# Forming the last output tile's sum in the matrix engine's banks, with its copies and stores on three engines

## The reference

```
x = x + rmsnorm(f, prm['ln_ffn_post'][i])
x = x + jax.nn.sigmoid(x @ prm['w_ple_gate'][i]) * (pe[i] @ prm['w_ple'][i])
```

## Time and profile before

| | us |
|---|---|
| median of 3 runs | 1069.44 (1069.35 to 1069.86) |
| the profiled execution's own time | 1069.43 |
| its span, first to last instruction | 1067.6 |
| PE busy in the span | 1057.3 |
| DVE busy | 671.6 |
| ACT busy | 550.6 |
| POOL busy | 216.2 |

### The profile page before, as it was taken

How to read it: one execution, slowest core, us unless ns; L and a number is a source line. 1 busy time by engine, 2 the same in 40 slices (tenths; PEclk the granted TensorE clock), 3 DMA queues, 4 the chain that set the end, 5 groups by cost and what they waited for, 6 DMA issues and landing times.

```text
span 1067.6 us, 20384 instructions
## 1 busy us (share of the span) xinstructions
PE 1057.3 (99%) x7347; PEld 1041.7 (98%) x7347; DVE 671.6 (63%) x1236; ACT 550.6 (52%) x940; POOL 216.2 (20%) x348
## 2 busy tenths in 40 slices
PE   8999999999999999999999999999999999999998
PEld 8889999999999999999999999999999999999998
DVE  6876557777777753333977665657777777433365
ACT  6565475555555543335666545655555555433353
POOL 7300022222322320002200102212223322110000
PEclk9999999999999999999999999999999999999999
DMA  9623253555555555545454344366555554545532
GB/s 258 171 72 88 89 158 102 163 157 161 153 151 145 153 148 153 149 148 159 120 158 127 102 125 135 94 136 170 160 156 144 151 157 142 152 145 156 156 101 70
DMA packets 281926, 150.39 MB, mean 141 GB/s; under 512 B 5592, under 2 KB 278816, under 8 KB 281872
## 3 DMA queue, kind: packets, MB, share of 16 engines
q1 hardware_dynamic: 279184, 144.20, 48.0%
q0 software_dynamic: 2544, 5.40, 1.7%
q10 hardware_dynamic: 144, 0.05, 0.0%
HBM read 145.54 MB, written 4.08 MB: 140 GB/s over the span
## 4 chain that ended last, share of the span: by engine, by line
PE 94%; DVE 2%; ACT 2%; DMA 1%; issue 1%; SPq 0%; DVEq 0%; ACTq 0%
PE bank L658 27%; PE bank L660 27%; PE bank L659 27%; PE bank L685 3%; PE bank L688 1%; PE bank L698 1%; PE bank L1029 1%; DMA raw<-in_w_att_in 1%; ACT wh L1177 1%; DVE wl L1504 1%; PE bank L931 1%; PE bank L1070 0%; PE bank L714 0%; PE bank L1072 0%; PE bank L1071 0%
## 5 line engine op out<-in xcount | busy, mean ns | idle before, releaser
L1504 DVE TENSOR_TENSOR wl<-raw,wh 128x1024 fp32r<-128x1024 f32 x270 | 332.4, 1231 | 253.3 <-ACT wh L1177 251.0
L658 PE MATMUL bank<-hH,wh 128*128 128x320 f32 x1280 | 399.5, 312 | 0.2
L660 PE MATMUL bank<-hH,wl 128*128 128x320 f32 x1280 | 395.5, 309 | 0.0
L659 PE MATMUL bank<-hL,wh 128*128 128x320 f32 x1280 | 395.4, 309 | 0.0
L1177 ACT ACTIVATE wh<-raw 128x1024 fp32r<-128x1024 f32 x270 | 284.6, 1055 | 167.5 <-PE bank L660 158.1
L658 PEld LDWEIGHTS bank<-hH,wh 128*128 128x128 f32 x1280 | 240.3, 188 | 1.3 <-issue 0.4
L659 PEld LDWEIGHTS bank<-hL,wh 128*128 128x128 f32 x1280 | 240.4, 188 | 0.2
L660 PEld LDWEIGHTS bank<-hH,wl 128*128 128x128 f32 x1280 | 240.2, 188 | 0.0
L658 PE MATMUL bank<-hidden_hi,wh 128*128 128x320 f32 x720 | 223.5, 310 | 0.5 <-ACT mix L1381 0.5
L660 PE MATMUL bank<-hidden_hi,wl 128*128 128x320 f32 x720 | 222.5, 309 | 0.0
L659 PE MATMUL bank<-hidden_lo,wh 128*128 128x320 f32 x720 | 222.5, 309 | 0.0
(11 more groups left out here) (371 smaller groups left out, 1028.4 us busy)
## 6 DMA issues: line engine op xcount, KB each, us to landing
raw<-in_w_ffn_up SPq DMA_DIRECT2D x128, 512.0 KB, 4.1
raw<-in_w_ffn_down SPq DMA_DIRECT2D x64, 512.0 KB, 4.0
raw<-in_w_rec_in SPq DMA_DIRECT2D x24, 512.0 KB, 3.9
raw<-in_w_att_in SPq DMA_DIRECT2D x18, 512.0 KB, 5.0
raw<-in_w_ple_gate SPq DMA_DIRECT2D x16, 512.0 KB, 4.0
raw<-in_w_att_out SPq DMA_DIRECT2D x8, 512.0 KB, 3.8
raw<-in_w_rec_out SPq DMA_DIRECT2D x8, 512.0 KB, 4.0
raw<-in_w_ple SPq DMA_DIRECT2D x4, 512.0 KB, 3.6
```

Source lines behind the costliest of these rows:

```text
L658: mmul(out, a, rh[:, k, :], start=first, stop=False)
L659: mmul(out, a, rl[:, k, :], start=False, stop=False)
L660: m = mmul(out, b, rh[:, k, :], start=False, stop=last)
L1504: V.tensor_tensor(wl[:, u % R, :], raw[:, u % R, :], wh[:, u % R, :].bitcast(F32), ALU.subtract).then_inc(lo_ready, 1)
```

## The change

The last tile's sum is no longer formed by DVE in `xT`. PE now multiplies the residual `xT[:, 7, ...]` by the identity into a bank and leaves the group open, then multiplies the gated product `sgb[:, 1, ...]` by the identity into the same places with accumulation, so that the bank holds the turned sum. The addition of line 1979 falls away for that one tile. The tile is split into two groups with banks of their own: `("y_end", 0)`, the prompt part, in bank 4, and `("y_end", 1)`, the sample part, in bank 5. DVE copies the prompt part and SP stores it; ACT copies the sample part, waits for its own copy and stores it from its own queue. The sample store of `turn_y(1)`, which SP issued, goes to POOL.

The diff is cut to its core; its pieces stand in the order PE, ACT, DVE, SP, POOL.

```
-            gi = gid("y_end")
-            bank_free(pe, gi)
-            pe.wait_ge(sem("x_out1"), 8)
-            for t, (t0, n) in enumerate(TOK):
-                m = trans(gbank(gi)[0:n, t * P:(t + 1) * P], xT[:, 7, t0:t0 + n], ident[:])
-            m.then_inc(done(gi), 1)
+            parts = (gid("y_end", 0), TOK[:2]), (gid("y_end", 1), TOK[2:])
+            for gi, tokens in parts:
+                bank_free(pe, gi)
+                for t, (t0, n) in enumerate(tokens):
+                    mmul(gbank(gi)[0:n, t * P:(t + 1) * P], xT[:, 7, t0:t0 + n], ident[:], start=t == 0, stop=False,
+                         skip_group_check=True)
+            pe.wait_ge(sem("sg"), 16)
+            for gi, tokens in parts:
+                for t, (t0, n) in enumerate(tokens):
+                    m = mmul(gbank(gi)[0:n, t * P:(t + 1) * P], sgb[:, 1, t0:t0 + n], ident[:], start=False, stop=True,
+                             skip_group_check=True)
+                m.then_inc(done(gi), 1)
...
+                        if i == 7:
+                            gi = gid("y_end", 1)
+                            bank_full(act, gi)
+                            A(xtok[0:TS, 2, 896:D], gbank(gi)[0:TS, 0:P], ACT.Copy).then_inc(sem("y_end_sample"), 1)
+                            act.wait_ge(sem("y_end_sample"), 1)
+                            act.dma_start(O["y_sample"][0, :, 896:D], xtok[0:TS, 2, 896:D]).then_inc(sem("y_stored"), 16)
...
-                    V.tensor_tensor(xT[:, i, :], xT[:, i, :], sgb[:, i % 2, :], ALU.add).then_inc(sem(f"x_out{l}"), 1)
+                    if l == 0 or i < 7:
+                        V.tensor_tensor(xT[:, i, :], xT[:, i, :], sgb[:, i % 2, :], ALU.add).then_inc(sem(f"x_out{l}"), 1)
...
-                for t in range(3):
+                for t in range(3 - half):
...
-            sp.wait_ge(sem("y_end"), 2)
-            sp.dma_start(O["y_sample"][0, :, 896:D], xtok[0:TS, 2, 896:D]).then_inc(sem("y_stored"), 16)
...
+            pool.wait_ge(sem("ytok"), 6)
+            pool.dma_start(O["y_sample"][0, :, y_columns(1)], xtok[0:TS, 2, y_columns(1)]).then_inc(sem("y5_stored"), 16)
+            pool.wait_ge(sem("y5_stored"), 16)
```

More of the change, by code:

```diff
@@ L126, in group_order @@
         o += [(f"gate{l}", i) for i in range(8 if l == 0 else 7)]
-    return o + [("y", 0), ("y", 1), ("y", 2), ("gate1", 7), ("y", 3), ("y", 4), ("y", 5), ("y_end", 0)]
+    return o + [("y", 0), ("y", 1), ("y", 2), ("gate1", 7), ("y", 3), ("y", 4), ("y", 5), ("y_end", 0), ("y_end", 1)]
 GROUPS = {key: n for n, key in enumerate(group_order())}
@@ L137, in group_banks @@
     fixed.update({("o", s): 7 for s in range(8)})
+    fixed.update({("y_end", 0): 4, ("y_end", 1): 5})
     fixed.update({(f"ple{l}", i): 4 + i for l in range(2) for i in (2, 3)})
@@ L462, in _ @@
                     sp.dma_start(dst[:, c], xtok[0:TOK[t][1], t, c]).then_inc(sem("y_stored"), 16)
-            sp.wait_ge(sem("y_end"), 1)
+            sp.wait_ge(sem("y_end_prompt"), 1)
             sp.dma_start(O["y_prompt"][0, :, 896:D].rearrange("(t p) c -> p t c", p=P), xtok[:, 0:2, 896:D]).then_inc(sem("y_stored"), 16)
-            sp.wait_ge(sem("y_end"), 2)
-            sp.dma_start(O["y_sample"][0, :, 896:D], xtok[0:TS, 2, 896:D]).then_inc(sem("y_stored"), 16)
-            sp.wait_ge(sem("y_stored"), 16 * 8)
+            sp.wait_ge(sem("y_stored"), 16 * 7)
         @block.gpsimd
@@ L1984, in _ @@
                     lo(UNITS[f"gate{l}"] + i + R)
-            gi = gid("y_end")
+            gi = gid("y_end", 0)
             bank_full(dve, gi)
-            V.tensor_copy(xtok[:, 0:2, 896:D], gbank(gi)[:, 0:2 * P].rearrange("p (t c) -> p t c", t=2)).then_inc(sem("y_end"), 1)
-            V.tensor_copy(xtok[0:TS, 2, 896:D], gbank(gi)[0:TS, 2 * P:3 * P]).then_inc(sem("y_end"), 1)
+            V.tensor_copy(xtok[:, 0:2, 896:D], gbank(gi)[:, 0:2 * P].rearrange("p (t c) -> p t c", t=2)).then_inc(sem("y_end_prompt"), 1)
 _OUTS = [
```

## The result

The changed kernel takes 1073.18 us (median of 7 runs, 1073.09 to 1073.22), the kernel before 1069.44 in the same session (7 runs, 1069.26 to 1070.07). The ratio is 1.0034, with a 95% interval of 1.0024 to 1.0043: slower by 3.74 us, or 0.34%. The forecast was 1068.7 and the top of its range 1069.8. The span of the profiled execution grew from 1067.6 to 1071.3, so all of the loss lies inside the span.

The account below looks back on a forecast made before the run. PE bounds the kernel, so only the 4.27 us tail behind its last gate matmul can change; last landing 1066.5 plus 0.36 gives span 1066.86, 0.74 less, time about 1068.7, range 1068.1 to 1069.8.

Parts of the forecast that it names:

- the sentence on POOL's store: Moved sample store of tiles 4 to 6: starts at 1064.23, lands at 1066.33, its wait holding up only the program's end.
- SP's 0.36: Program's end: 0.36 us from the last landing to the span's end, taken from the kernel before.
- The 0.17 for the shared transfer engines: Last stores: sharing 16 transfer engines puts the last landing at 1066.5, where the queues alone gave 1066.33.
- The cover holds but for 0.02 us: PE behind the gate: three residual matmuls fit before the product arrives, costing only 0.02 us.
- the 0.113: PE's last tile: step in us of one plain matmul, taken to be the same as a transpose's.
- POOL's store becomes the last: Rival, program's end: a POOL flight of 3.4 to 4.2 lands last, time 1069.8 to 1070.6; range 1069.0 to 1070.6, chance 0.17.
- its deciding point of 3.0: POOL's moved store: a flight of 3.0 us or more costs the whole gain.
- The plain matmuls are slow: Rival, PE's last tile: plain matmuls at four times the transposes' pace, step 0.45 us, time 1070.3; chance 0.06.
- ACT's store is the late one: Rival, last sample store: an ACT flight of 2.95 us from 1064.29 leaves the time at 1069.4; chance 0.07.
- The addition's place: Chain behind the gate: without DVE's sum, 0.54 us goes and PE could start on the product 0.14 after its end.
- POOL's flight of 2.1: Moved store of tiles 4 to 6: 2.1 us from issue to landing, as SP's 96 KB store took.
- Slower by over 0.2%: Whole kernel: needs a POOL flight of over 5.1 us or several rivals together; chance 0.04.

Follow-up runs that it names:

- The kernel with separate transposes: Changed kernel with residual and product each turned by transposes, DVE adding the product, sample store of tiles 4 to 6 on SP: 1069.85 against 1069.54 us, ratio 1.0001.

## Why the prediction was wrong

**The sum was made up to the wrong end.** The step that failed is the sentence on POOL's store: "Nothing else stands behind its wait in POOL's stream, so that holds up only the program's end." The program's end is just what was being predicted, and a DRAIN of 4.3 us stands behind that wait. The sum went from the last landing to the end by SP's 0.36, which is the price of SP's closing. POOL's closing has another, and its row, 5.0 us at 1013.0 with 0.8 of an operation in it, was in the trace of before. It wasn't read, since in a kernel whose POOL ends 50 us early it decides nothing. By it the sum would have been: POOL's landing as forecast, 1066.33, plus 0.15 and 0.3 (as in the profile after) and 4.2 to 5.0 between them, a span of 1071.0 to 1071.8 and a time of 1072.8 to 1073.6; 1073.18 was measured. The 0.17 for the shared transfer engines played no part in the answer: of the three last stores POOL's landed first, and the end hung on it.

**The residual matmuls don't hide.** "The cover holds but for 0.02 us" failed by its size: they hold PE for some 0.6 beyond the product's arrival. The pace in the earlier trace rows was read per row count, six in 0.83, and that count is of instructions. The code at that line issues three matmuls a pass, so the 0.113 is the step of half a matmul, and a whole one steps by 0.23. In the trace after, the three take PE from 1063.11 to 1064.01, 0.30 each; the step from 0.23 to 0.30 is not explained. This ate the 0.54 of the addition, and the product's own matmuls, 1.07 where the transposes took 0.53, put the prompt's copy 0.27 later than before.

**The rivals.** *POOL's store becomes the last* had the engine right and the mechanism wrong: the flight was 2.1, as taken, its deciding point of 3.0 was not reached, and the store landed ahead of the other two; what was late is what comes after the landing. *The plain matmuls are slow* held in its mechanism, and the point that it gave, a step of 0.3, is what was measured: there "the sample store starts at 1065.4, as before", and it started at 1065.42. Its price of four times the pace didn't come. The rule of the Trainium skill, "TensorE: Matmul & The Clock Gate", section Terms, that the transpose mode is four times as fast for FP32 on trn2, points the right way; here a matmul of this size took 0.30 against 0.11 for a transpose, 2.7 times. *ACT's store is the late one*: its flight was 1.9 and not 2.95, so no; it landed last of the three because it started at 1065.42 and not at 1064.29.

**What held.** The addition's place: without the residual's matmuls, PE starts on the product 0.16 after its end (0.14 forecast). POOL's flight of 2.1 held to the row, its start came 0.56 after ACT's last copy (1063.89 to 1064.45) and not 0.30 as in the earlier trace rows, which put its landing 0.22 later than forecast. The 0.17 for the shared transfer engines was not put to the test: the last stores started late, the engines were busy for only 0.05 of 1065.10 to 1065.50, where the forecast had no gap, and the three flights were 1.8, 2.1 and 1.9, against 1.8, 2.1 and 1.8. The Trainium skill, "DMA: Bandwidth & Descriptors", section "Issuing engines are not separate DMA queues", says that transfers started by several engines interleave on the same DMA engines. The kernel with separate transposes fits it: there SP's and ACT's sample stores started 0.52 and 0.19 ahead of the prompt's, which flew for 2.3 and not 1.8.

**The range and the chances.** Slower by over 0.2% had 0.04, on the ground that it needed a flight of POOL's over 5.1. The bound was on the wrong term: a price that no row of the end showed, the closing of an engine that had never closed last, was taken as the one that SP's row showed.

**What stays open.** What POOL does in its DRAIN was not tried, nor whether it is as long in a program in which POOL starts no transfers at all. The difference between POOL's start of 0.30 at 409 us and 0.56 at the end wasn't followed either; with 0.55 to 0.57 in the three other kernels that give POOL a store, it isn't scatter. Nor was it tried what makes the flight of the prompt's store 1.8 in some kernels and 2.1 or 2.3 in others. No version was faster than the kernel before by more than the medians scatter.

## What to carry to other kernels

Before work is moved to an engine that had finished early, read what that engine does at the program's close, and count it behind the moved work: here the close of POOL took 4.2 us and of SP 0.013. By these rows, as an estimate, POOL can take a store for nothing only if it lands some 4.8 us ahead of the end (0.15, 4.3 and the 0.3 of the meeting); the one that landed 5.4 ahead cost nothing. Count what a row counts: the nine extra instructions for three extra matmuls told that a float32 matmul by the identity is two instructions and a transpose one. And a gain on one engine at the very end is worth what the stores behind it leave of it: 0.48 us saved ahead of the last prompt store came out as nothing.

## What the runs showed of the hardware

- POOL's closing DRAIN ends 4.2 to 4.4 us behind POOL's last work, whatever that was: 4315 ns after a landing, 4233 after a bare wait, 4.35 us behind the issue of a store (a row of 4882 ns) and 4.2 behind an operation (a row of 5022 ns). SP's takes 0.013, ACT's 0.4 behind the issue of its store, and those of PE and DVE end about 0.1 behind their last work, which their rows of up to 1.78 include.
- A plain float32 matmul by the identity, 128 columns wide, is two instructions on PE and takes 0.30 us for the two at the program's end; a transpose of the same shape is one, at a step of 0.11.
- A wait at the block's end can stand under the wrong name: SP's 3.8 us of waiting are put down to PE, whose DRAIN ended at 1065.2, while POOL's ended at 1071.0.
- The flight of the last prompt store (128 KB, SP) was 1.8 us in the kernel before, 1.8 and 1.9 where ACT's 32 KB store started 0.14 and 0.15 behind it, 2.1 where ACT's started 0.04 ahead of it, and 2.3 where 96 KB of SP's and ACT's 32 KB started 0.52 and 0.19 ahead of it.
